# Choice rows to 128 partitions, attention's ends reordered, a twelfth expert slot and unread products in a decoder step

## The reference

```python
# token mixer
rq, rk, rv, rg, mq, mk, mv, ga, gb = split(x @ w_in)        # 7 groups of 512 columns, 2 gates of 1024
o_r = retention(rq, rk * 128**-0.5, rv)                      # 4 heads of 128, chunks of 128
o_r = silu(rg) * group_norm(o_r) * gn_g                      # per token and head
o_m = block_sparse_attention(mq, mk, mv)                     # 8 heads of 64; the sample also reads cached pages
merged = sigmoid(ga + b) * (o_r @ w_br_ret) + sigmoid(gb + b) * (o_m @ w_br_moba)
x1 = layer_norm(ALPHA * x + merged @ w_out, ln1_g, ln1_b)
# hierarchical mixture of experts, 4 groups of 8, hidden width 128
g = argmax(x1 @ w_rg + b_rg)                                 # one group per token
e_val, e_idx = top_k((x1 @ w_re[g] + b_re[g]), 2)            # two experts of that group
e_w = softmax(e_val) * softmax(group logits)[g]
hid = silu(x1 @ w_eg) * (x1 @ w_eu)
moe = sum over the two experts of e_w * (hid @ w_ed)
y = layer_norm(ALPHA * x1 + moe, ln2_g, ln2_b)
```

## Time and profile before

| | |
|---|---|
| Median of 3 runs | 690.81 us (689.77 to 691.32) |
| Profiled execution | 689.35 us, of which the span from first to last instruction is 687.5 |
| Mean granted TensorE clock | 0.949 |
| Busy share of the span | PE 89%, PEld 73%, DVE 45%, ACT 21%, POOL 11% |
| Moved by DMA | 124.43 MB, 181 GB/s over the span |

### The profile page before, as it was taken

How to read it: one execution, slowest core, us unless ns; L and a number is a source line. 1 busy time by engine, 2 the same in 40 slices (tenths; PEclk the granted TensorE clock), 3 DMA queues, 4 the chain that set the end, 5 groups by cost and what they waited for, 6 DMA issues and landing times.

```text
span 687.5 us, 10970 instructions
## 1 busy us (share of the span) xinstructions
PE 610.0 (89%) x4390; PEld 502.6 (73%) x4390; DVE 309.6 (45%) x602; ACT 143.4 (21%) x290; POOL 75.4 (11%) x78
## 2 busy tenths in 40 slices
PE   3999999999998798799999999999933999999863
PEld 2999999999975564699999998788732555554410
DVE  6344343444337568734445544464575122222126
ACT  0111011030155255310001112120111232322202
POOL 0101400021052000000000000000003122221114
PEclk9999999999998999989999999999955999999977
DMA  9425322136307435022333312595078799999195
GB/s 355 160 75 173 117 62 92 61 92 210 115 21 219 119 118 185 32 62 92 123 138 128 106 59 92 208 415 209 33 279 315 276 409 417 414 415 384 69 211 178
DMA packets 45977, 124.43 MB, mean 181 GB/s; under 512 B 6289, under 2 KB 19729, under 8 KB 41714
## 3 DMA queue, kind: packets, MB, share of 16 engines
q1 hardware_dynamic: 39888, 112.23, 46.1%
q0 software_dynamic: 4752, 8.93, 3.5%
q10 hardware_dynamic: 1298, 2.73, 1.0%
HBM read 114.62 MB, written 17.43 MB: 192 GB/s over the span
## 4 chain that ended last, share of the span: by engine, by line
PE 75%; DVE 8%; DMA 8%; issue 3%; ACT 3%; SPq 2%; POOLq 0%; DVEq 0%; ACTq 0%
PE ps L709 13%; PE ps L707 13%; PE ps L708 13%; PE ps L1035 6%; PE ps L702 6%; DMA scratch<-experts 3%; PE ps L1050 3%; DMA arena<-token_rows 3%; PE ps L926 2%; PE ps L983 2%; PE ps L928 2%; PE ps L927 2%; PE ps L985 2%; PE ps L984 2%; PE ps L769 1%
## 5 line engine op out<-in xcount | busy, mean ns | idle before, releaser
L707 PE MATMUL ps<-xa_hi,w_hi 128*128 128x272 f32 x704 | 205.8, 292 | 11.4 <-DVE xa_lo L1441 11.4
L709 PE MATMUL ps<-xa_hi,w_lo 128*128 128x272 f32 x704 | 204.4, 290 | 0.0
L708 PE MATMUL ps<-xa_lo,w_hi 128*128 128x272 f32 x704 | 203.8, 290 | 0.0
L707 PEld LDWEIGHTS ps<-xa_hi,w_hi 128*128 128x128 f32 x704 | 133.7, 190 | 12.7 <-issue 10.0
L708 PEld LDWEIGHTS ps<-xa_lo,w_hi 128*128 128x128 f32 x704 | 133.9, 190 | 0.0
L709 PEld LDWEIGHTS ps<-xa_hi,w_lo 128*128 128x128 f32 x704 | 133.6, 190 | 0.0
L1432 DVE CAST w_hi<-w_ring 128x1024 fp32r<-128x1024 f32 x52 | 37.9, 729 | 114.3 <-PE ps L709 85.0
L1434 DVE TENSOR_TENSOR w_lo<-w_ring,w_hi 128x1024 fp32r<-128x1024 f32 x52 | 65.7, 1263 | 1.8
L1035 PE MATMUL ps<-arena,work 128*64 128x256 f32 x384 | 49.7, 394 | 2.9 <-ACT work L1269 2.2
L1374 POOL DMA_INDIRECT work<-x_rows,idx_i x13 | 13.3, 1027 | 343.3 <-DVE idx_i L1814 312.9
L1035 PEld LDWEIGHTS ps<-arena,work 128*64 128x64 f32 x384 | 29.8, 141 | 17.6 <-ACT work L1269 2.9
(11 more groups left out here) (263 smaller groups left out, 874.6 us busy)
## 6 DMA issues: line engine op xcount, KB each, us to landing
w_ring<-w_tiles SPq DMA_DIRECT2D x52, 512.0 KB, 3.5
arena<-experts SPq DMA_DIRECT2D x24, 1024.0 KB, 13.9
arena<-experts SPq DMA_DIRECT2D x24, 512.0 KB, 16.9
arena<-kT_pool SPq DMA_DIRECT2D x16, 256.0 KB, 3.1
out<-arena SPq DMA_DIRECT2D x4, 1024.0 KB, 5.4
arena<-v_pool SPq DMA_DIRECT2D x16, 256.0 KB, 2.9
arena<-token_rows SPq DMA_DIRECT2D x8, 512.0 KB, 11.3
cst<-experts SPq DMA_DIRECT2D x3, 1024.0 KB, 23.0
```

What stands on the lines that cost most here:

```text
L707: mm(out, w_hi[b][:, w], x_hi[:, k_x, cols], start=start, stop=False)
L708: mm(out, w_hi[b][:, w], x_lo[:, k_x, cols], start=False, stop=False)
L709: return mm(out, w_lo[b][:, w], x_hi[:, k_x, cols], start=False, stop=stop)
```

## The change

*Order of the groups.* RQ comes before MQ. DVE, not ACT, takes RQ out of PSUM and multiplies it by its decay, so POOL's four decay products go. A fill of 26 products of a block of ones (written by DVE first of all) stands ahead of TensorE's first tile; nobody reads it.

*End of attention.* The high part of the first two gate tiles moves to ACT (`high_parts`), the second tile gets a third pair of split buffers over constants that are no longer needed and comes earlier in `ORDER`; the scaling of the retention rows moves to ACT (`scaled_rows`), with DVE multiplying by the gate after it; the transposes of the rows become jobs X in the list, ahead of the last attention products, each with a PSUM bank of its own.

*Routing.* Unread products of the identity (17, 17 and 20) stand ahead of the ranks, ahead of the slot products and behind them. The rank matrices move into space of `work` and are copied by ACT later.

*Experts.* There are 12 slots; the twelfth lies over x1 tiles 0 to 2. SP issues experts 3 to 6 after the last x1 tile, waits for the first gather, the x1 transposes and the x1 stores, and then issues the experts of slots 7 and 11. When 12 pairs are through their down products it fetches the three x1 tiles back from memory and then loads the rows of layer norm 2.

*Choice rows.* One load takes both choices of 64 tokens, to 128 partitions; the two halves of a tile are two loads, and the sample tile is one.

The diff, cut to its core:

```diff
-SLOTS = 11
+SLOTS = 12
-MK, RK, RV, RG, MV, MQ, RQ = range(7)
+MK, RK, RV, RG, MV, RQ, MQ = range(7)
...
-                        w_ring[:, :, :].rearrange("p a n -> p (a n)")[:, 0:EW])[s - 8]
+                        w_ring[:, :, :].rearrange("p a n -> p (a n)")[:, 0:EW], arena[:, 0:EW])[s - 8]
...
                  + moba(3) + O("pv", 2) + [("T", ("samp", 1)), ("N", ("std",)), ("W", (0,))] + inv(3) + O("sampv", 1)
-                 + [("N", ("rows",))] + turned(3) + O("sel", 1) + [("G", (0,))] + O("pv", 3))
+                 + turned(3) + [("N", ("rows",)), ("W", (1,))] + O("sel", 1) + [("G", (0,))]
+                 + [("X", (t,)) for t in range(TT)] + O("pv", 3) + [("G", (1,))])
...
+        def w_buf(m):
+            return 2 if m == 1 else m % 2
+        def x_bank(t):
+            return (4, 5, 2, 3, 6 + (O_IDX[("pv", 3)] + 1) % 2)[t]
...  (SP)
-            for s in range(3, 8):
+            for s in range(3, 7):
                 load_parts(s, experts_d[s])
-            sp.dma_start(ln_g, ln2_g.partition_broadcast(P)).then_inc(s_ln2, 16)
-            sp.dma_start(ln_b, ln2_b.partition_broadcast(P)).then_inc(s_ln2, 16)
+            sp.wait_ge(s_gx[0], 16)
+            sp.wait_ge(s_x1t, TT)
+            sp.wait_ge(s_x1s, 16 * TT)
+            for s in (7, 11):
+                load_parts(s, experts_d[s])
...
             refill_down(10)
+            sp.wait_ge(s_dn, 12)
+            sp.dma_start(x_tm[:, 0:3], x1_d[0:3 * P].rearrange("(t p) n -> p t n", p=P)).then_inc(s_x, 16)
+            sp.dma_start(ln_g, ln2_g.partition_broadcast(P)).then_inc(s_ln2, 16)
+            sp.dma_start(ln_b, ln2_b.partition_broadcast(P)).then_inc(s_ln2, 16)
...
-                for c in range(2):
-                    rows = rows_d[c * T + t * P:c * T + t * P + r]
-                    if t < 4:
-                        sp.dma_start(picked[c * CAP:(c + 1) * CAP, t], rows.rearrange("(g p) n -> p g n", g=2)
-                                     ).then_inc(s_yg[t], 16)
-                    else:
-                        sp.dma_start(x_tm[(c + 1) * NS:(c + 2) * NS, t, :], rows).then_inc(s_yg[t], 16)
+                both = rows_d[0:2 * T].rearrange("(c x) n -> c x n", c=2)[:, t * P:t * P + r]
+                if t < 4:
+                    for g in range(2):
+                        sp.dma_start(picked[:, t, g], both[:, g * CAP:(g + 1) * CAP]).then_inc(s_yg[t], 16)
+                else:
+                    sp.dma_start(x_tm[NS:3 * NS, t, :], both).then_inc(s_yg[t], 16)
...  (TensorE)
+            pe.wait_ge(s_on, 1)
+            for _ in range(26):
+                mm(ps[:, 7, 0:P], lg_s[:, 0:P], lg_s[:, 0:P], start=True, stop=True)
...
+            def turn_rows(t):
+                pe.wait_ge(s_gn, t + 1)
+                if t < 2:
+                    pe.wait_ge(s_tu, nT)
+                elif t < 4:
+                    pe.wait_ge(s_su, nS)
+                else:
+                    pe.wait_ge(s_ou, done("sel", 1))
+                b = x_bank(t)
+                ... transposes into bank b
...
+            def stay_active(n):
+                for _ in range(n):
+                    mm(ps[:, 3, 0:P], ident, ident, start=True, stop=True)
+
+            stay_active(17)
             pe.wait_ge(s_msk, 1)
...
+            stay_active(17)
             for n in range(2 * TT):
...
             m.then_inc(s_ohu, 1)
+            stay_active(20)
...
+            pe.wait_ge(s_x, 48)
             for t in range(4):
                 for half in range(2):
                     mm(ps[:, 2 * t + half, :], scaled_id, x_tm[:, t, half * 512:(half + 1) * 512], start=True, stop=True,
...  (ACT)
+            def high_parts(m):
+                act.wait_ge(s_o, max(done("reto", 3), done("cross", 1)))
+                act.wait_ge(s_s, used(("samp", 1)))
+                act.wait_ge(s_w[m % 4], 16 * (8 + m // 4))
+                A(w_hi[w_buf(m)][:], w_ring[:, m % 4, :], ACT.Identity).then_inc(s_hi, 1)
+            def scaled_rows():
+                act.wait_ge(s_gnm, 1)
+                for t in range(4):
+                    for h in range(RH):
+                        o = rk_t[:, t, h * P:(h + 1) * P]
+                        n = 4 * h + t
+                        m = A(o, o, ACT.Identity, scale=gstd[:, n:n + 1], bias=gmv[:, n, 0:1])
+                    m.then_inc(s_nr, 1)
...  (POOL)
-            for h in range(RH):
-                q = fm[:, 4 * FM_OF[RQ] + h, 0:NP].rearrange("p (c n) -> p c n", c=4)
-                m = pv.tensor_tensor(q, q, C("qdec")..., ALU.mult)
-            m.then_inc(s_qd, 1)
...  (DVE, while tiles 20 to 23 are projected)
+                    v.tensor_tensor(q[:, 0:HALF], ps[:, b, 0:HALF], decay, ALU.mult)
+                    v.tensor_tensor(q[:, HALF:NP], ps[:, b + 1, 0:NP - HALF], decay[:, skip:skip + NP - HALF], ALU.mult)
+                    v.tensor_copy(q[:, NP:T], ps[:, b + 1, NP - HALF:HALF]).then_inc(s_pev, 1)
...
             def split_tile(m):
-                if m == 0:
-                    dve.wait_ge(s_o, max(done("reto", 3), done("cross", 1)))
-                    dve.wait_ge(s_s, used(("samp", 1)))
-                elif m == 1:
+                if m < 2:
+                    dve.wait_ge(s_hi, 28 + m + 1)
+                    v.tensor_tensor(w_lo[w_buf(m)][:], w_ring[:, m % 4, :], w_hi[w_buf(m)][:].bitcast(F32), ALU.subtract
+                                    ).then_inc(s_spl, 1)
+                    return
+                if m == 3:
                     dve.wait_ge(s_o, done("pv", 3))
```

More of the change, by code:

```diff
@@ L227, in hybrid_step @@
         xg = [work[:, 0:1024], work[:, 1024:2048], w_ring[:, 3, :], work[:, 7168:8192]]
+        w_hi2, w_lo2 = under(CO["cmask"][0], [("w_hi2", [P, D]), ("w_lo2", [P, D])])
+        assert CO["cmask"][0] + 2 * D <= CO["sdecay"][0]
         cst = sb("cst", [P, NCONST])
@@ L884, in gate @@
                 b = 0 if kind == "a" else 2
-                project_split(m % 2, b, 0, xa_hi, xa_lo)
-                project_split(m % 2, b + 1, 1, xa_hi, xa_lo).then_inc(s_tile, 1)
+                project_split(w_buf(m), b, 0, xa_hi, xa_lo)
+                project_split(w_buf(m), b + 1, 1, xa_hi, xa_lo).then_inc(s_tile, 1)
+            def turn_rows(t):
[7 more added lines that the diff above has]
+                b = x_bank(t)
+                if t < 4:
+                    for c in range(4):
+                        m = tr(ps[:, b, c * P:(c + 1) * P], rg_t[:, t, c * P:(c + 1) * P], P)
+                else:
+                    m = tr(ps[:, b, 0:P], xs, P)
+                m.then_inc(s_ot, 1)
             for kind, jb in ORDER:
@@ L896, in _ @@
                     gate(jb[0])
[L899 to L906, removed]
-                    for c in range(4):
-                        m = tr(ps[:, b, c * P:(c + 1) * P], rg_t[:, t, c * P:(c + 1) * P], P)
-                else:
-                    m = tr(ps[:, b, 0:P], xs, P)
-                m.then_inc(s_ot, 1)
+                elif kind == "X":
+                    turn_rows(jb[0])
             def branches(m):
@@ L1090, in _ @@
                     pe.wait_ge(s_cen, 1)
-                pe.wait_ge(s_yg[t], 32)
+                pe.wait_ge(s_yg[t], 32 if t < 4 else 16)
                 for half in range(2):
@@ L1135, in _ @@
             A(rg_t[0:NS, 4, :], rg_t[0:NS, 4, :], ACT.Silu).then_inc(s_sig, 1)
-            for g in (MQ, RQ):
-                for j in range(4):
-                    act.wait_ge(s_proj, 4 * g + j + 1)
-                    A(fm[:, 4 * FM_OF[g] + j, :].rearrange("p (h c) -> p h c", h=2),
-                      ps[:, 2 * (j % 2):2 * (j % 2) + 2, 0:HALF], ACT.Identity,
-                      scale=DH ** -0.5 if g == MQ else 1.0).then_inc(s_pev, 1)
+            act.wait_ge(s_pev, 2 + 4 * MQ)
+            for j in range(4):
+                act.wait_ge(s_proj, 4 * MQ + j + 1)
+                A(fm[:, 4 * FM_OF[MQ] + j, :].rearrange("p (h c) -> p h c", h=2),
+                  ps[:, 2 * (j % 2):2 * (j % 2) + 2, 0:HALF], ACT.Identity, scale=DH ** -0.5).then_inc(s_pev, 1)
             act.wait_ge(s_par, 64)
@@ L1196, in _ @@
                     A(gstd[:], gmv[:, :, 1], ACT.Sqrt, bias=C("eps")).then_inc(s_gsq, 1)
+                elif kind == "W":
+                    high_parts(jb[0])
+                elif kind == "X":
+                    turned_rows(jb[0])
+                elif (kind, jb) == ("N", ("rows",)):
+                    scaled_rows()
             def gate_values(m):
@@ L1205, in gate_values @@
                   bias=bm[:, 8 * u + n:8 * u + n + 1]).then_inc(s_cgs, 1)
-            for t in range(TT):
-                act.wait_ge(s_ot, t + 1)
-                b = t_bank(nT + t)
-                cols = slice(t * P, (t + 1) * P) if t < 4 else slice(NP, T)
-                r = P if t < 4 else NS
-                A(o_r[:, R_HI:R_HI + 4, cols], ps[:, b, 0:4 * r].rearrange("p (c n) -> p c n", c=4), ACT.Identity
-                  ).then_inc(s_otc, 1)
-                if t == 0:
-                    gate_values(0)
```

(5 more changed lines are left out.)

88 lines of the change are left out of this document (49 added, 39 removed).

## The result

The changed kernel takes 742.78 us (742.43 to 745.53), the kernel before 690.37 beside it: ratio 1.077, 95% interval 1.0737 to 1.0796. The profiled execution is 742.62 us with a span of 740.8.

What follows compares the result with a forecast made beforehand. TensorE bounds the kernel (75% of the span), so only its idle or half-clock places give time back. -2.0 - 4.3 - 4.0 - 3.5 + 65.5 = +51.7; 689.35 + 51.7 + 1.5 gives 742 us, range 666 to 752.

Steps and rivals of the forecast that it cites:

- Choice rows: Final choice-row loads: a source of two blocks gets two DMA engines, so the end comes 65.5 us later.
- The lower of the two bounds: Choice-row load rate: one engine to a block, 51.5 GB/s, against an upper end of 412 GB/s.
- My reading: Choice-row loads: engines are dealt by the outermost dimension, read from old 64-partition loads keeping all 16 engines busy.
- Routing: Routing to first expert pair: fills keep the clock up and the gather runs alone; gain 4.0 us, bounds 1.4 and 6.
- none is late: Routing fills of 17, 17 and 20 products (4.1, 4.9 us) fit into TensorE's idle 6.36, 5.11 and 7.54 us.
- Twelfth slot: Expert stream: 20 instead of 21 experts remain for the crowded part; gain 3.5 us, bounds 0 and 4.4.
- named against this step: Twelfth slot: a wait of the scaled x1 products for their fetch would make the step wrong.
- End of attention: High parts and scalings to ACT, turned rows behind the first gate tile: gain 4.3 us, bounds 1.5 and 6.
- 4.3 + 1.8 - 1.8 = 4.3: End of attention: 4.3 us of waiting gone, 1.8 from clock and transposes (1.5, 0.3), less 1.8 for late inversions.
- Head: Head of attention: quicker DVE scalings without POOL's decay products, shorter TensorE gap; gain 2.0 us, bounds 0 and 3.5.
- Start: Start: 26 unread products are worth 0, since x's last piece sets the time; bounds 0.3 either way.
- the 1.5 added for the median: End of the sum: the median shown, 690.81 us, lies 1.46 above the profiled execution of 689.35.

Runs made afterwards that it cites:

- Experiments 1 to 4: Choice-row loads as before in the changed kernel, 677.89 us; token outermost there, 672.58; source of four blocks there, 699.81; only the new loads in the kernel before, 754.13.
- 5: Changed kernel with the choice rows' source token outermost (672.58 us), without the three routing fills: 671.26 us.
- 8: Experiment 6's version without the hold, slots 7 and 11 no longer waiting for the first gather: 670.38 us.
- 7: Changed kernel with the choice rows' source token outermost (672.58 us), with 11 expert slots and no fetch of x1 tiles: 672.65 us.
- Experiment 6: Changed kernel with the choice rows' source token outermost (672.58 us), first gate tile's high part made by DVE again: 667.98 us.
- 11: Experiment 6's version, hold kept, plus five unread products among the last scores and slot 7's gate and up part sent before the hold: 664.81 us.
- 12: The version of 11 without the 26 unread products at the start and the write that feeds them: 667.13 us.
- 10: The version of 8 with five unread products in TensorE's wait among the last attention scores: 669.79 us.
- experiment 1: Changed kernel with the choice rows loaded as before, 64 partitions and one choice a load: 677.89 us, ratio 0.982.

## Why the prediction was right, and where it was not

- *Choice rows.* Of +53.3 they are +63.6; 65.5 was said. The lower of the two bounds, far apart as they were, held: 52.5 GB/s instead of 51.5, which makes 1.6 of the difference of 1.9; the flow started 3.0 us after its first issue, as said. Experiments 1 to 4 show the cause. "My reading" of the 64-partition loads, that the outermost dimension deals the engines, holds for 2, 4 and 64.
- *Routing.* -4.0 as said, but not in the parts that were said. That the fills bring the clock up is shown by 5 (3.2 us in their stretch), that the hold keeps the gather quick by 8. But the price of a fill was read too low: 17 products took 6.13 us and 20 took 7.53, where 4.1 and 4.9 were said. So "none is late" failed for the third fill, which ran past the gather's landing: the transposes came 5.3 us after the gather's issue, before 5.6, and not 4.2. The clock gave the rest. What the sum didn't see: in the traces of 5 such a gain was lost again at the experts' stream.
- *Twelfth slot.* -3.0 against -3.5. The fetch was late by 1.44 us as was named against this step, but the scatter and the choice loads cover it. Whether the slot itself brings this is not settled (7).
- *End of attention: the step that failed.* The sum had "4.3 + 1.8 - 1.8 = 4.3", with 1.5 as its lower bound; 0.4 came. The 1.8 of late inversions was right (1.6), and the order won even more than said: from the first to the second gate tile 12.72 us instead of 16.02 though 22 products ran at half clock (2.2), and 1.2 behind it, 6.7 together. What the sum left to its lower bound is the clock: with 2.30 us of waiting instead of 0.71 it fell, 1.56 in the transposes and 2.2 in the gate tile. Experiment 6 took the longer wait away, and the clock stayed. All six traces with the longer wait lost the clock there; of the eight with the short one six kept it, but 11 and 12 did not. So the longer wait isn't the only way to lose it, and what decides is open. Another 1.5 was lost at the scores (3.56 instead of 2.02), where I had not looked; 10, 11 and 12 show that a fill prevents it at that place. Ahead of the scores 0.6 was won that the sum did not have.
- *Head: a term too small.* 3.8 instead of 2.0, above its bound of 3.5. The wait fell from 3.08 to 0.74, since POOL's masks came near the end of the first scalings, not beside them, and with the clock up the transposes took 4.24 instead of 5.71.
- *Start.* +0.95 in this trace against 0, outside the 0.3 given. x's last piece came 0.3 later (16.16, before 15.85), and its first six products at half clock cost the other 0.6. That the clock could fall again between the pieces was left out. It did in eight of the eleven traces with the fills (granted clock from 10 to 20 us 0.68 to 0.83); these end the projections at 197.0 to 198.4. The three in which it stayed up (1.00) end them at 196.3 to 196.6, three without the fills at 196.6, 197.1 and 197.6. In these traces, then, the fills pay only where the clock lasts to the last piece.

The errors (+0.95, -1.8, +3.9, +0.5, -1.9) cancel to 1.6. The forecast was right because its largest term was right. That it met the median within 1 us is luck: the errors cancel, and of the 1.5 added for the median only 0.2 came (742.78 against 742.62).

## What to carry to other kernels

Before reshaping a load to reach more partitions, write out the access pattern of both sides and look at the outermost size: if it is small, turn the order so that a long dimension comes first, even if the weights or masks downstream must follow. A wait that an edit makes longer is to be priced with the clock behind it, since the products after it can cost more than the wait (here 3.8 us behind 1.6). And a gain ahead of a saturated stream has to be checked behind it, for it can be lost there again.

## What was not expected of the hardware

- SP was blocked while it issued: eight loads over two engines held its queue 52.96 us, over sixteen 5.22 us in experiment 1. The sample tile's load behind them went out only at 695.38.
- TensorE's clock fell in a wait of 1.30 us among the scores in eight of nine traces of the changed front without a fill there (granted clock from 255 to 265 us 0.83), and stayed up in the same wait in the ninth (1.00) and in both with the old front. The wait's length alone does not tell, as 11 and 12 show for the inversions too.
- 64-partition loads kept all 16 engines busy (share 1.03) at 220 GB/s, loads to 128 partitions of the same rows moved 378 at a share of 0.96: the share alone does not tell the rate.
